# Where the operands of TensorE's products begin in SBUF: seven groups of buffers move from 0 or 128 to 64 modulo 256 bytes

## What is computed

```python
def swiglu(u, wg, wu, wd):
    return (jax.nn.silu(u @ wg) * (u @ wu)) @ wd
...
for l in range(DEPTH):            # DEPTH = 2, first block
    h = h + 0.5 * swiglu(rmsnorm(h, g_pre[l]), ...)
    h = h + mixer(rmsnorm(h, g_mix[l]))      # pooling for l = 0, MLA for l = 1
    h = h + 0.5 * swiglu(rmsnorm(h, g_post[l]), ...)
    if l == 0:
        k_nope, k_rope, v = mla_shared_kv(h, ...)
```

## The kernel before

| buffer | role in the products | start modulo 256 before |
|---|---|---|
| hiA, loA, hiB, loB | stationary or moving | 128 |
| h, xs | stationary | 128 |
| xh, xl | moving, or stationary in `by_tokens` | 64 |
| act_s, act_h, act_hh, act_hl | the last two stationary in down | 128 |
| row_gain, cols, ident, ident_r, mask_r | ident moving in roots and transposes | 128 |
| ckvh, ckvl, k_rope, cqh, cql | moving in MLA | 128 |
| oh2, ol2 | moving in the third stage, stationary in MLA's output | 0 |
| arena | all scratch of the mixers | 0 |

## Time and profile before

### The profile page before, as it was taken

One profiled execution on the slowest core, in us unless ns is written; L12 is line 12 of the kernel. 1 busy time (PEld: TensorE's weight loads), 2 busy tenths in 40 slices (PEclk: granted clock), 3 DMA queues, 4 the chain that ended last, 5 costly groups with the idle time before them and its releaser, 6 DMA issues.

```text
span 1950.0 us, 33841 instructions
## 1 busy us (share of the span) xinstructions
PE 1915.1 (98%) x13298; PEld 1776.2 (91%) x13298; DVE 1228.7 (63%) x1650; ACT 944.3 (48%) x1295; POOL 55.8 (3%) x90
## 2 busy tenths in 40 slices
PE   9999999999999999999999999999999999999998
PEld 8999999999998888999899998899989998879997
DVE  6655765575545646655666689665566665876655
ACT  5444544454445645444544458644454446445443
POOL 0000100000000000000100000100000000010000
PEclk9999999999999999999999999999999999999999
DMA  7555355445453135555544432655545453344552
GB/s 278 195 194 194 137 194 194 183 172 185 183 194 130 66 127 198 193 193 190 199 184 180 164 141 101 235 194 194 186 162 195 183 193 116 130 149 168 190 194 97
DMA packets 61216, 338.81 MB, mean 174 GB/s; under 512 B 6816, under 2 KB 7200, under 8 KB 32736
## 3 DMA queue, kind: packets, MB, share of 16 engines
q1 hardware_dynamic: 59184, 330.00, 45.7%
q0 software_dynamic: 1968, 7.93, 1.2%
HBM read 336.85 MB, written 1.05 MB: 173 GB/s over the span
## 4 chain that ended last, share of the span: by engine, by line
PE 91%; DVE 4%; ACT 2%; issue 1%; POOL 1%; DMA 0%; SPq 0%; DVEq 0%; ACTq 0%; POOLq 0%
PE X L1545 57%; PE Y L1545 33%; ACT hiA L545 1%; DVE xl L1054 1%; DVE loA L1027 1%; DVE h L1097 0%; PE X L1579 0%; DVE xs L1090 0%; ACT xh L585 0%; DVE arena L1338 0%; DMA cols<-in_cols 0%; POOL rstd L445 0%; PE Y L1926 0%; PE X L1577 0%; DVE h L1081 0%
## 5 line engine op out<-in xcount | busy, mean ns | idle before, releaser
L1545 PE MATMUL X<-xh,hiA 128*128 128x256 f32 x2592 | 732.3, 283 | 5.8 <-DVE loA L1013 3.0
L1545 PE MATMUL X<-xl,hiA 128*128 128x256 f32 x2592 | 729.0, 281 | 0.0
L1545 PE MATMUL X<-xh,loA 128*128 128x256 f32 x2592 | 728.8, 281 | 0.0
L1027 DVE TENSOR_TENSOR loA<-rawA,hiA 128x2048 fp32r<-128x2048 f32 x220 | 504.1, 2291 | 272.4 <-ACT hiA L545 272.0
L1545 PEld LDWEIGHTS X<-xh,hiA 128*128 128x128 f32 x2592 | 488.4, 188 | 14.4 <-DVE loA L1013 3.8
L1545 PEld LDWEIGHTS X<-xh,loA 128*128 128x128 f32 x2592 | 498.1, 192 | 0.0
L1545 PEld LDWEIGHTS X<-xl,hiA 128*128 128x128 f32 x2592 | 488.6, 189 | 5.5
L545 ACT ACTIVATE hiA<-rawA 128x2048 fp32r<-128x2048 f32 (+1 forms) x234 | 423.3, 1809 | 57.9 <-PE Y L1545 30.7
L1545 PE MATMUL Y<-hiB,act_hh 128*128 128x512 f32 x704 | 274.7, 390 | 0.0
L1545 PE MATMUL Y<-hiB,act_hl 128*128 128x512 f32 x704 | 274.4, 390 | 0.0
L1545 PE MATMUL Y<-loB,act_hh 128*128 128x512 f32 x704 | 274.3, 390 | 0.0
(11 more groups left out here) (242 smaller groups left out, 2064.5 us busy)
## 6 DMA issues: line engine op xcount, KB each, us to landing
rawA<-in_wa SPq DMA_DIRECT2D x221, 1024.0 KB, 5.5
rawB<-in_wb SPq DMA_DIRECT2D x181, 512.0 KB, 3.5
row_gain<-in_rows POOLq DMA_DIRECT2D x8, 512.0 KB, 6.4
arena<-in_gla POOLq DMA_DIRECT2D x1, 1280.0 KB, 10.1
h<-in_x SPq DMA_DIRECT2D x2, 512.0 KB, 4.0
out<-h SPq DMA_DIRECT2D x2, 512.0 KB, 2.6
arena<-in_pool POOLq DMA_DIRECT2D x1, 768.0 KB, 4.9
arena<-in_taps POOLq DMA_DIRECT2D x1, 576.0 KB, 4.3
```

Of the source, the lines that this page charges most:

```text
L1027: nc.vector.tensor_tensor(loA[p][:, :], rawA[p][:, :], hiA[p][:, :].bitcast(f32), ALU.subtract).then_inc(a_lo, 1)
L1545: return say(nc.tensor.matmul(*args, **kw))
```

## The change

The filler `half_line` grows from 8 to 56 elements (32 to 224 bytes in each partition), and the filler `half_line_2` of 128 bytes goes. No instruction is added, removed or moved, and no engine's program changes but in addresses. `act_s`, `act_h`, `act_hh`, `act_hl` and all that follows them up to `cql` begin 192 bytes later, at 64 modulo 256 instead of 128. `oh2`, `ol2` and `arena` begin 64 bytes later, at 64 instead of 0. What stands before the filler keeps its place: all weight tiles, `h`, `xs`, `xh` and `xl`.

```diff
@@ -119,7 +119,7 @@
         xh = sb("xh", [P, KD, TOKENS], f32r)
         xl = sb("xl", [P, KD, TOKENS], f32r)
         flag = sb("flag", [P, 2])
-        half_line = sb("half_line", [P, 8])
+        half_line = sb("half_line", [P, 56])
         act_s = sb("act_s", [P, 2, TOKENS])
         act_h = sb("act_h", [P, 2, TOKENS])
         act_hh = sb("act_hh", [P, 2, TOKENS], f32r)
@@ -134,7 +134,6 @@
         k_rope = sb("k_rope", [P, 2, TOKENS])
         cqh = sb("cqh", [P, 2, TOKENS], f32r)
         cql = sb("cql", [P, 2, TOKENS], f32r)
-        half_line_2 = sb("half_line_2", [P, 32])
         oh2 = sb("oh2", [P, 8, TOKENS], f32r)
         ol2 = sb("ol2", [P, 8, TOKENS], f32r)
         arena = sb("arena", [P, 15384])
```

## The result

The changed kernel took 1924.99 us (median of 4 runs, 1921.83 to 1928.04), the kernel before 1949.43 (4 runs, 1948.88 to 1951.57). The ratio is 0.9872 with a 95% interval of 0.9854 to 0.9891. The forecast was 1921. The profiled execution took 1925.92 us with a span of 1924.1, against 1951.95 and 1950.0 before: 26.0 us less.

What follows compares the result with a forecast made beforehand. TensorE's product pitch was taken as the bound. Seven stages 21.2 less 0.5 and 0.3, third stage 6.1 + 0.3, MLA 1.1 + 0.3 make 28.2 us less: 1921 us, own range 1914 to 1928, 8-in-10 range 1916 to 1955.

Steps and rivals of the forecast that it cites:

- The deciding point: Feed-forward loops: down groups at (moving 128, stationary 64) hand gate and up products the fast pace, 113.3 instead of 117.8 ns.
- the prediction's own sign: Feed-forward loops: prediction is wrong if a (128, 64) down group hands over the slow pace, or a new third pace appears.
- between the two streams of reads: TensorE in the second stage: the two paces of (64, 128) are a phase, entered by a disturbance at `roots` and kept.
- the 0.5 us in the sum: Seven stages' openings: 15 products each already run fast before `roots`, so 0.5 us of the gain is not to be had.
- The new step: Feed-forward loop: 48 gate and up products 5.44, 12 down products 2.75, handovers 0.04, together 8.23 us instead of 8.374.
- the 0.04 us for the handovers: Each feed-forward step: slower products on leaving the down group, and the same again, estimated, on the way into it.
- The third stage: Third feed-forward stage: step falls from 8.52 to 8.23 us, 6.1 us less, plus 0.3 us from 48 first products.
- MLA: MLA: 240 products with cqh, cql, ckvh, ckvl moving save 1.1 us; 156 output products going to (128, 64) save 0.3 us.
- Rival 2: Feed-forward loops: fast handover only in some stages or for one loop parity; about 13 us less, 1936 us; chance 0.12.
- Rival 1: Seven stages: slow pace stays and down groups cost 30 ns more each; 1952 us, within 1950 to 1955; chance 0.32.
- Rival 3: Only the moving operand's start matters: down stays 226.7 ns, third stage saves 3.2 us, MLA 0.8; 1945.3 us; chance 0.10.
- Rival 4: Whole kernel: the starts have no effect, as the skill's rule of two independent read ports implies; 1949.3 us; chance 0.04.

Runs made afterwards that it cites:

- the kernel with the act buffers alone: Kernel before with only act_s, act_h, act_hh, act_hl moved to 64 modulo 256, all other buffers at their old starts: 1931.87 us, ratio 0.9908.
- the kernel with (192, 128): Changed kernel with down weights hiB, loB at 192 (h, xs too) and act at 128, so down is (moving 192, stationary 128): 1952.55 us, ratio 1.001.
- the kernel with the others alone: Changed kernel with the four act buffers left at 128 and everything behind them at 64: 1946.47 us, ratio 0.9978.

## Why the prediction was right

- That TensorE's pitch is all that counts, and that no other engine would take over: right. VectorE's busy time is the same to 0.1 us, the taps still take 479 ns.
- The deciding point, that a down group at (128, 64) hands over the fast pace: right for seven of eight stages, and shown by the kernel with the act buffers alone. By the prediction's own sign, that it is wrong if such a group hands over to the slow pace, it failed in the fourth. It rested on one place, and that this place was enough was in part luck: the kernel with (192, 128) shows that the neighbours of the pair count as well, and in the earlier trace rows they happened to be the ones of the loop.
- The phase "between the two streams of reads" is not shown. That a disturbance enters the slow pace and that it is then kept was read from the head of the second stage; the sixth stage of the kernel before ran at 118 ns already ahead of `roots`, so not every opening is fast, as the 0.5 us in the sum took for granted. And it is not the roots that hold the loops slow in the kernel before, but the down groups.
- The new step: 8.23 us forecast, 8.21 measured. Down at 229.2 ns was right (2.75 us); of the 0.04 us for the handovers 0.02 was there, the five products behind the down group (5.47 instead of 5.44 us), and the way into it cost nothing.
- The third stage: 8.52 to 8.23 forecast, 8.21 measured, and the reading of its 2.76 us as a leftover is shown by the kernel with the others alone.
- MLA: the stretch between the third and the fourth stage fell by 0.7 us, not 1.4, since part of the products with `cqh` run at 117.8 and not at 113.3 ns. Its 156 output products went from 36.06 to 35.72 us, the 0.3 forecast. The place of `ident` made no difference that was seen.
- Rival 2 had the mechanism of one stage, though not its 1936 us: the fourth kept the slow pace and lost 173.4 - 169.3 = 4.1 us, which is most of what separates 1925 from 1921. That the loop "forgets how it began" was the argument against it; for (128, 128) it is true, for (128, 64) not. The runs of the changed kernel spread over 6.2 us, those of before over 2.7. Runs with none, one or two slow stages would lie 4.1 us apart; only single executions have a trace here, so this is argued and not shown. The spread is weak evidence too: over the 20 executions beside the first experiments the kernel before spread over 4.0 us. The rival also took the third stage to be without such products; it has two of its own, recorded as four, at 414.26 us in the trace after. The alternation that it named, a loop with both paces, came with the act buffers at 192 and at 0.
- Rival 1 describes that fourth stage (5.65 us, and 2.77 where it put about 2.75). Rival 3 fell with the step of 8.21. Rival 4 fell: 256 columns cost 113.3, 117.8 or 120 ns by how the starts of the two operands relate and by what ran before. The Trainium skill, page "TensorE: Matmul & The Clock Gate", section "Step-by-step: what each phase is for", says that loading the next weights takes no SBUF read bandwidth from the running matmul; it gives no reason for these differences, and whether they come from the reads at all no run shows.

What stays open: why the starts matter at all. The runs show that moving one group of buffers against the others by 64 bytes changes the pace, that moving all of them by 64 bytes does not, and that a pace outlasts hundreds of products; they do not show a mechanism, nor whether SBUF or TensorE sets it. It is also open what exactly at a stage's start picks the rhythm.

## What to carry to other kernels

When TensorE is the bound and its products follow each other without waits, divide groups of equal products by their count and compare the pitches between stages: a stage that is faster and differs only in addresses points at a gain that costs a few bytes of filler. Try the starts of moving and stationary operands as a set, on the chip, since neither 64 as such nor one pair's difference predicts the rest. Where the executions of a new layout spread more than those of the old one, as with down at (64, 128) (14.5 us over seven executions), look for stages that fell into different rhythms.

## What the runs showed that I had not expected

- Shifting all buffers by 64 bytes left every group's time the same (5.65, 2.72, 5.76, 2.76 us).
- A loop can alternate between the paces tile by tile (5.46 and 5.66 us with act at 192).
- The cheapest down group is the worse choice. At (128, 128) and (192, 192) it takes 2.72 us (226.7 ns for 512 columns), against 2.75 at (128, 64), 2.77 at (128, 0) and 2.80 at (128, 192). It costs 0.03 us less than at (128, 64), and the gate and up group behind it 0.18 more (5.65 instead of 5.47).
- A down group at (128, 192) or (128, 0) turns over the pace that it gets, one at (128, 128) makes it slow, one at (128, 64) makes it fast in most cases.
- The pace can stay with a loop for 19 measured steps in a row in one stage and be another in the next, with the same code and the same starts.
